# Keys and values of both attention branches as one 512-column product, and an indexer whose queries 1 to 3 are taken from rounded planes

## What is computed

```python
qa, ka, va, qb, kb, vb, iq, ik, iw, ga, gb = jnp.split(jnp.dot(h, w_in), IN_SPLITS, axis=-1)
dots = jnp.einsum('bqhd,bsd->bqhs', iq, ik) * IDX_SCALE
score = jnp.einsum('bqh,bqhs->bqs', iw * IDX_HEAD_SCALE, jax.nn.relu(dots))
_, sel = lax.top_k(score, topk)          # then attention b over the selected keys
```

## Time and profile before

| | us |
|---|---|
| median of three runs | 1031.42 |
| lowest and highest | 1030.24, 1037.22 |
| the profiled execution, its device time | 1036.8 |
| its span (first to last instruction) | 1035.0 |
| PE busy | 925.9 (89%) |
| DVE busy | 378.2 (37%) |
| ACT busy | 256.5 (25%) |
| mean granted clock of TensorE | 0.967 |

### The profile page before, as it was taken

The page is one execution under the profiler, slowest core; times in us unless marked ns, Lnnn a source line. Parts: engine busy times, 40 slices in busy tenths (PEclk is TensorE's granted clock), DMA queues, the critical chain, the costliest instruction groups (busy, mean ns, idle before and its releaser), DMA issues.

```text
span 1035.0 us, 14155 instructions
## 1 busy us (share of the span) xinstructions
PE 925.9 (89%) x5699; PEld 591.2 (57%) x5702; DVE 378.2 (37%) x974; ACT 256.5 (25%) x523; POOL 132.4 (13%) x136
## 2 busy tenths in 40 slices
PE   7989999999999999998999977877887888887996
PEld 7869995456999998994333322322322222234775
DVE  4179996764233436453111101101101011102796
ACT  6244326764323233221000000000000000001542
POOL 2403701113030000001111110011010110000000
PEclk9999998999999999997999999999999899999998
DMA  9850602002834316366999999999999999996601
GB/s 265 118 152 2 203 1 62 1 2 68 263 105 120 78 46 244 128 236 239 427 427 425 427 428 428 424 428 425 429 426 426 427 426 425 427 428 264 254 22 66
DMA packets 60132, 263.72 MB, mean 255 GB/s; under 512 B 11054, under 2 KB 36030, under 8 KB 46224
## 3 DMA queue, kind: packets, MB, share of 16 engines
q1 hardware_dynamic: 54160, 250.99, 63.0%
q0 software_dynamic: 5296, 9.79, 2.6%
q10 hardware_dynamic: 624, 2.23, 0.6%
HBM read 253.99 MB, written 16.85 MB: 262 GB/s over the span
## 4 chain that ended last, share of the span: by engine, by line
PE 63%; DMA 29%; DVE 4%; ACT 2%; issue 1%; SPq 1%; DVEq 0%; ACTq 0%
DMA arena<-in_w_up 25%; PE ps L1111 13%; PE ps L1278 12%; PE ps L980 5%; PE ps L1143 4%; PE ps L1426 4%; PE ps L1303 3%; PE ps L881 3%; PE ps L952 3%; DMA arena<-in_w_ple 2%; PE ps L1044 2%; PE ps L1014 2%; PE ps L1065 2%; PE ps L1399 1%; PE ps L1172 1%
## 5 line engine op out<-in xcount | busy, mean ns | idle before, releaser
L1278 PE MATMUL ps<-arena,hT 128*64 128x512 f32 x960 | 234.5, 641 | 39.4 <-DMA arena<-in_w_up 39.2
L1278 PEld LDWEIGHTS ps<-arena,hT 128*64 128x64 f32 x960 | 71.6, 141 | 199.3 <-issue 149.4
L2211 DVE TENSOR_TENSOR xf<-xf,ps 128x256 f32<-128x256 f32 x32 | 13.5, 421 | 401.6 <-ACT xf L1699 379.1
L1111 PE MATMUL ps<-arena_merge,arena_merge 128*128 128x256 f32 x624 | 99.7, 287 | 0.0
L1303 PE MATMUL ps<-arena,xf 128*64 128x512 f32 x336 | 76.7, 598 | 12.8 <-DVE xf L2214 12.8
L1111 PEld LDWEIGHTS ps<-arena_merge,arena_merge 128*128 128x128 f32 x624 | 87.4, 188 | 0.0
L836 POOL DMA_INDIRECT expert_rows<-xf,arena x32 | 32.2, 1007 | 425.6 <-ACT xf L1703 399.8
L1111 PE MATMUL ps<-xf_merge,arena_merge 128*128 128x256 f32 x480 | 82.0, 288 | 0.0
L1699 ACT ACTIVATE xf<-ps 128x256 f32<-128x256 f32 x30 | 11.6, 385 | 259.1 <-PE ps L1278 259.1
L1111 PEld LDWEIGHTS ps<-xf_merge,arena_merge 128*128 128x128 f32 x480 | 69.3, 188 | 0.0
L1703 ACT ACTIVATE xf<-ps 128x512 f32<-128x512 f32 x30 | 17.9, 598 | 159.8 <-PE ps L1303 159.8
(11 more groups left out here) (309 smaller groups left out, 1311.1 us busy)
## 6 DMA issues: line engine op xcount, KB each, us to landing
arena<-in_w_gate SPq DMA_DIRECT2D x30, 2048.0 KB, 29.4
arena<-in_w_up SPq DMA_DIRECT2D x30, 2048.0 KB, 37.0
arena<-in_w_down SPq DMA_DIRECT2D x11, 2048.0 KB, 36.4
hT<-in_w_down SPq DMA_DIRECT2D x11, 2048.0 KB, 36.5
arena<-in_w_down SPq DMA_DIRECT2D x20, 1024.0 KB, 32.2
arena<-in_w_in SPq DMA_DIRECT2D x10, 1024.0 KB, 6.2
arena<-in_w_in SPq DMA_DIRECT2D x3, 2048.0 KB, 10.5
arena<-in_w_gate SPq DMA_DIRECT2D x8, 512.0 KB, 9.0
```

Source lines behind the costliest of these rows:

```text
L1111: mm = pe.matmul(w[:, 2 * lo_t:lo_t + hi_t], rounded(st[:, c, cols]), rounded(mv[:, c, lo_t:hi_t]), start=c == 0 and k == 0, stop=c == pla ...
L1278: mm = pe.matmul(ps[g * BLK:(g + 1) * BLK, 2 + s, :], xsT[:, c, col:col + BLK], expert_columns(k, slice(0, 2), c, g), start=c == 0, stop=c ...
```

## The change

1. `iq` 1 to 3 are made in rounded planes (`index_queries` on PE) instead of float32. ACT makes their three high planes (`iq_hi`) ahead of that of `kvb`, and POOL their low planes. `iq` 0 stays a float32 product.
2. The order is now `iq` 0, `ikw`, `iq` 1, `ikT` p, `iq` 2, `ikT` s, `iq` 3, `dots`, on all engines. The first `dots` waits for `iq` 3 instead of `ikT` s.
3. ACT makes the high plane of `kva` between its readings of `ikT` s and of `iq` 3, instead of behind the dots. SP loads `kva` as soon as `ikw` is full, ahead of `qb`.
4. Keys and values of both branches are one product of 512 columns per tile, with one ring use (`('kv', t)`) instead of two. ACT reads a tile in two instructions. The sample's sums stand behind the second tile. PE waits for ACT's last tile once, and then makes all four groups of transposes.
5. ACT makes the high planes of `qb` ahead of its readings of the `kv` tiles, not behind the keys of branch b.

```diff
-    [(('xT', t), 'dve') for t in range(TILES)] + [(('iq', m), 'dve') for m in range(4)]
-    + [(('ikT', s), 'dve') for s in 'ps']
+    [(('xT', t), 'dve') for t in range(TILES)] + [(('iq', 0), 'dve'), (('iq', 1), 'dve'), (('ikT', 'p'), 'dve')]
+    + [(('iq', 2), 'dve'), (('ikT', 's'), 'dve'), (('iq', 3), 'dve')]
...
-    + [(('kvb', t), 'act') for t in range(TILES)] + [(('kva', t), 'act') for t in range(TILES)], 2)
+    + [(('kv', t), 'act') for t in range(TILES)], 2)
...
+    iq_hi = [None] + [at(kb, [KD, P]) for kb in (97.25, 101.25, 105.25)]
+    kv_lo2, kv_hi2 = at(16, [2, KD, 256]), at(32.5, [2, KD, 256])
...
+        sp.wait_ge(narrow_full, NARROW[('ikw', 4)].fill)
+        load(slab_kva, w_in[:, :, C_KVA:C_KVA + 256], slab_in['kva'])
         sp.wait_ge(wide_full, WIDE[('iq', 3)].fill)
         load(slab[0], w_in[:, :, C_QB:C_QB + 512], slab_in['qb'])
-        sp.wait_ge(wide_full, WIDE[('ikT', 'p')].fill)
-        load(slab_kva, w_in[:, :, C_KVA:C_KVA + 256], slab_in['kva'])
-        sp.wait_ge(narrow_full, NARROW[('kva', 4)].fill)
+        sp.wait_ge(narrow_full, NARROW[('kv', 4)].fill)
         load(slab[1], w_in[:, :, C_QA:C_QA + 512], slab_in['qa'])
...
-        pool.wait_ge(sw_high, 1)
+        for m in range(1, 4):
+            pool.wait_ge(sw_high, m)
+            low_of(slab[0][:, :, m * P:(m + 1) * P], slab[0][:, :, m * P:(m + 1) * P], iq_hi[m], "front").then_inc(sw_split, 1)
+        pool.wait_ge(sw_high, 4)
         low_of(slab_kvb, slab_kvb, kv_hi['b'], "front").then_inc(sw_split, 1)
+        pool.wait_ge(sw_high, 5)
+        low_of(slab_kva, slab_kva, kv_hi['a'], "front").then_inc(sw_split, 1)
...
+        def index_queries(m):
+            w = wide(open_slot(WIDE, ('iq', m), wide_out))
+            pe.wait_ge(f_split, KD)
+            for k in range(3):
+                if k == 2:
+                    pe.wait_ge(sw_split, m)
+                for c in range(KD):
+                    st = slab[0][:, c, m * P:(m + 1) * P] if k == 2 else iq_hi[m][:, c, :]
+                    mv = hT_lo if k == 1 else hT_f
+                    for a in range(2):
+                        mm = pe.matmul(w[:, a * 512:a * 512 + HALF], rounded(st, "front"),
+                                       rounded(mv[:, c, a * HALF:(a + 1) * HALF]),
+                                       start=c == 0 and k == 0, stop=c == KD - 1 and k == 2)
+            mm.then_inc(wide_full, 1)
+
+        pe.wait_ge(sw_high, 3)
+        index_queries(1)
...
-        pe.wait_ge(wide_out['dve'], WIDE[('ikT', 's')].out)
+        index_queries(3)
+        pe.wait_ge(wide_out['dve'], WIDE[('iq', 3)].out)
...
+        pe.wait_ge(sw_split, 5)
+        for t in range(TILES):
+            slot = open_slot(NARROW, ('kv', t), narrow_out)
+            for c in range(KD):
+                for k, (st, mv) in enumerate(((hT_f, kv_hi2), (hT_f, kv_lo2), (hT_lo, kv_hi2))):
+                    mm = pe.matmul(by_half(ps[0:ROWS[t], 6 + slot, :]), rounded(st[:, c, tok(t)]), rounded(mv[:, :, c, :], "front"),
+                                   start=c == 0 and k == 0, stop=c == KD - 1 and k == 2)
+            mm.then_inc(narrow_full, 1)
+            if t == 1:
+                sample_sums()
+        pe.wait_ge(narrow_out['act'], NARROW[('kv', 4)].out)
...
+        act.wait_ge(slab_in['iq'], 16)
+        for m in range(1, 4):
+            high(iq_hi[m], slab[0][:, :, m * P:(m + 1) * P], "front").then_inc(sw_high, 1)
         act.wait_ge(slab_in['kvb'], 16)
         high(kv_hi['b'], slab_kvb, "front").then_inc(sw_high, 1)
...
+        index_keys('s', NP, PAST + NS)
+        act.wait_ge(slab_in['kva'], 16)
+        high(kv_hi['a'], slab_kva, "front").then_inc(sw_high, 1)
+        index_queries(3)
...
-        act.wait_ge(slab_in['kva'], 16)
-        high(kv_hi['a'], slab_kva, "front").then_inc(sw_high, 1)
+        act.wait_ge(slab_in['qb'], 16)
+        query_weights_high(slab[0], qb)
+        for t in range(TILES):
+            slot, r = close(NARROW, ('kv', t), narrow_full), ROWS[t]
+            act.activation(kv_b[0:r, t, :], ps[0:r, 6 + slot, 256:512], ACT.Copy)
+            act.activation(kv_a[0:r, t, :], ps[0:r, 6 + slot, 0:256], ACT.Copy).then_inc(narrow_out['act'], 1)
```

More of the change, by code:

```diff
@@ L767, in query_weights_low @@
                 low(s[:, 4:8, m * P:(m + 1) * P], q_hi(dst, m, 1), "front").then_inc(sw_split, 1)
-        query_weights_low(3, slab[0], qb)
-        pool.wait_ge(narrow_out['act'], NARROW[('kvb', 4)].out)
+        query_weights_low(6, slab[0], qb)
+        pool.wait_ge(narrow_out['act'], NARROW[('kv', 4)].out)
         for nm, c in (('new_k', 0), ('new_v', P)):
@@ L909, in _ @@
         pe.wait_ge(wide_out['dve'], WIDE[('xT', 4)].out)
-        for m in range(4):
-            slot = open_slot(WIDE, ('iq', m), wide_out)
-            project(slot, lambda c: slab[0][:, c, m * P:(m + 1) * P], P, None, 0).then_inc(wide_full, 1)
+        slot = open_slot(WIDE, ('iq', 0), wide_out)
+        project(slot, lambda c: slab[0][:, c, 0:P], P, None, 0).then_inc(wide_full, 1)
         pe.wait_ge(slab_in['ikw'], 16)
@@ L945, in _, with sample_sums @@
         pe.wait_ge(f_split, KD)
[L946 to L960 removed]
+        def sample_sums():
+            w = wide(open_slot(WIDE, 'sums', wide_out))
+            pe.wait_ge(relu_used, 3 * HEADS + KV)
+            for lo, hi in ((0, PAST), (PAST, PAST + NS)):
+                mm = pe.matmul(w[0:NS, lo:hi], ident_s, score_s[:, lo:hi], start=True, stop=True)
+            mm.then_inc(wide_full, 1)
+        pe.wait_ge(sw_split, 5)
[9 more added lines that the diff above has]
+        pe.wait_ge(narrow_out['act'], NARROW[('kv', 4)].out)
+        for br, kv_n in (('b', kv_b), ('a', kv_a)):
             w = wide(open_slot(WIDE, ('k' + br + 'T', 'p'), wide_out))
[L962 removed]
             for t in range(4):
@@ L1888, in _, with index_keys @@
             ins.then_inc(wide_out['dve'], 1)
+        def index_keys(i, part, lo, cols):
+            w = wide(close(WIDE, ('ikT', part), wide_full))
+            dve.wait_ge(ik_high, i + 1)
+            dve.tensor_tensor(rounded(ikT[:, lo:lo + cols], "front"), w[:, 0:cols],
+                              rounded(ik_hi[:, lo:lo + cols], "front").bitcast(F32), ALU.subtract).then_inc(wide_out['dve'], 1)
+        index_queries(0)
         for t in range(TILES):
@@ L1896, in _ @@
             dve.tensor_scalar(iw_n[0:r, t, :], src[:, HD:IKW], IW_SCALE, None, ALU.mult).then_inc(narrow_out['dve'], 1)
-        for i, (part, lo, cols) in enumerate((('p', 0, NP), ('s', NP, PAST + NS))):
-            w = wide(close(WIDE, ('ikT', part), wide_full))
-            dve.wait_ge(ik_high, i + 1)
-            dve.tensor_tensor(rounded(ikT[:, lo:lo + cols], "front"), w[:, 0:cols],
-                              rounded(ik_hi[:, lo:lo + cols], "front").bitcast(F32), ALU.subtract).then_inc(wide_out['dve'], 1)
+        index_queries(1)
+        index_keys(0, 'p', 0, NP)
+        index_queries(2)
+        index_keys(1, 's', NP, PAST + NS)
+        index_queries(3)
         dve.wait_ge(narrow_out['dve'], NARROW_DONE['dve'])
```

45 lines of the change are left out of this document (11 added, 34 removed).

## The result

| | before | changed |
|---|---|---|
| median of 11 runs, us | 1035.39 | 1043.10 |
| lowest and highest, us | 1030.24, 1038.30 | 1039.38, 1046.89 |
| span of the profiled execution, us | 1035.0 | 1041.1 |
| mean granted clock of TensorE | 0.967 | 0.956 |

The changed kernel is slower: the ratio of its time to the time before is 1.0087, with a 95% interval of 1.0065 to 1.0109, so 9.0 us (6.7 to 11.3). The forecast was 1035.5 us, in a range of 1029.0 to 1040.5.

What follows compares the result with a forecast made beforehand. Up to attention, PE's and DVE's chains from the first dots were taken to bound it, 0.73 us apart. Dots 4.8 us later put attention +4.1 us: 1031.42 + 4.1 = 1035.5 us, range 1029.0 to 1040.5.

Steps and rivals of the forecast that it cites:

- The sum: DVE's chain at 165.9 us releases attention instead of at 161.84, +4.1 us, with nothing behind it changed.
- The wait for kva: ACT before reading iq 3: kva lands at 61.8 us behind the store, so dots start at 66.6, 4.8 us later.
- Rival A: SP's load of kva passes the store and lands before 55.4 us; attention 2.2 us early, 1029.2 us; chance 0.12.
- B: Rival: kva lands only at 66.8 us, dots 9.8 us late, attention 9.1, total 1040.5 us; chance 0.08.
- kva's low plane on POOL ends near 68.3, before kv at 84.: POOL's low plane around the start of dots, counted as free because keys and values need it only later.
- The small stall: PE inside ikw waits about 1.4 us for a narrow slot, vanishing in the wait for kva.
- The planes: Indexer queries iq 1 to 3 on PE: 6.06 us each instead of 7.38, saving 4.0 us, lost in PE's wait.
- The dots: Indexer dots stage: paced by DVE, low clock before too, length taken as unchanged.
- rival C: PE's wait costs TensorE's clock, sample's dots 4 us longer, 1039.5 us; slower by over 1% if longer; chance 0.05.
- Keys and values: PE's 512-column products behind the dots: 27.3 us instead of 28.66, gain 1.4 us, 1.1 after an added wait.
- D: Rival: the wide keys-and-values product gains nothing, attention +4.8 us, 1036.2 us; chance 0.75 together with the main forecast.
- The base: Whole kernel: the difference was put on the median 1031.42 us, the profiled execution being 0.5% above it.

Runs made afterwards that it cites:

- e6: Changed kernel, with the load of kva issued on ACT's queue at the same point, the store to toeplitz left on SP's queue; ratio to the kernel before 1.0087.
- e2: Changed kernel, with DVE's four small copies and the reduction moved ahead of its reading of iq 3; ratio to the kernel before 1.0046.
- e3: Changed kernel, with POOL's low plane of kva started only after DVE's first multiply-add on dots; ratio to the kernel before 1.0088.
- e4: e1 plus ACT reading iq 0 ahead of making the high plane of kvb; ratio to the kernel before 0.9978.
- e5: e4 plus DVE's copies moved behind its reading of ikT p, and dots started before iq 3 is read; 1031.20 us, ratio to the kernel before 0.9961.
- e8: Changed kernel, with only ACT's reading of iq 0 moved ahead of kvb's high plane, the store in its old place; one run, 1046.53 us.
- e1: Changed kernel, with SP issuing the store to toeplitz behind the loads of kva and qb; ratio to the kernel before 1.0024.
- e9: e5 with iq 1 to 3 as float32 products again, without their high and low planes; ratio to the kernel before 1.0008.
- e10: Kernel before the change, with DVE's four small copies and the reduction moved behind its last ikw tile; ratio to the unedited kernel 0.9999.
- a0: Changed kernel measured again without any edit, beside e1 to e3; 1044.09 us, ratio to the kernel before 1.0069.

## Why the prediction was off

**The effect, term by term.** The sum gave +4.1 us at attention, and +7.50 came. Of the 3.4 between them 0.9 are kva's later landing, 2.0 are DVE's copies, which had no term, and 0.5 are a gain behind the dots of which less came (0.3 us instead of 0.7). The range missed for one more reason, the base.

**The wait for kva: right, and 1.0 us short.** The prediction had kva land at 61.8 behind the store, ACT's high plane there, and dots at 66.6. They are 62.8 and 67.47, so +5.74 instead of +4.84. From kva's landing to the dots it gave 4.8 us and it took 4.66. The step that was short is the landing, worked out as 59.1 plus 2.7: the store landed at 59.3, and kva 3.4 us behind it, in other executions up to 4.4. Its reason, an order within the queue, is not needed, since another queue waits as long (e6); that the figure was near is in part luck. Rival A, that kva passes the store, is refuted; what it quotes is on the order of completion, not on a load that overtakes a store. B, a landing at 66.8, did not come.

**The failed step: "kva's low plane on POOL ends near 68.3, before kv at 84."** That asks only who needs the result, and costs the instruction at nothing. It ran from 64.80 to 69.31, and DVE had copies at 67.45. The trace before has them beside the first dots (61.59 and 61.73), so the prediction's own times, dots at 66.6 and POOL up to 68.3, laid one on the other. They took 2.73 us instead of 0.66, on DVE's chain and, through the dots, on PE's. The first multiply-add comes 3.13 us behind the first dots instead of 1.11: +2.02. With the 5.74 this is the whole +7.76. e2 and e3 show POOL as the cause; that 0.3 of it belong to POOL's issue of a store rather than to its low plane is read from the trace alone.

**The small stall: right in place, wrong in price, and hidden.** 1.4 us were forecast and 1.10 came. What it cost besides was a clock of 0.50 behind it: with the stall ikw takes 3.3 us longer than the 8.38 of e4, e5 and e8 (in e1 4.9), and the first instructions of iq 1 another 1.1. So PE was done with iq 3 at 59.88 and not at 57.3, and waited 7.59 us instead of 9. The prediction let it "vanish" in the wait for kva; in the changed kernel it does (e8), in a kernel where kva is in time it does not (e1 against e4).

**The planes: right.** 4.0 us forecast, 3.95 measured (e9 against e5), and in the changed kernel all of it lost in the wait.

**The dots, and rival C: right, refuted.** From first to last multiply-add it is 18.37 us before and after, although the granted clock was 0.50 up to about 75.8. The keys and values started at full rate. The measured time lies above C's 1039.5, but what C named did not bring it there.

**Keys and values: 1.4 us forecast, 0.45 came.** The 120 instructions of 512 columns take 11.33 + 16.88 = 28.21 us, 0.235 each, not the 0.227 of the earlier trace rows; before they took 28.66. From the first of them to the first of qb it is 32.09 us against 32.36, a gain of 0.27 instead of 1.1. The other traces agree: from the first multiply-add to attention it is 99.22 and 99.26 us with two products (before, e10) and 98.95 to 98.97 with one (the changed kernel, a0, e1, e4, e5, e6, e8, e9; in e2 and e3 POOL lies on multiply-adds of that stretch). D, put in the forecast's own range, was nearer. So PE's chain was again the longer one. DVE was done at 169.03 and ACT's last reading released the memset at 169.34, where the prediction had DVE release attention. That is why 7.76 at the scores became 7.50 at attention, and no less.

**The base.** The sum was put on a median of three runs, 1031.42. Eleven runs of the kernel before give 1035.39. Of the 7.6 us between forecast and result 4.0 are this, and 3.6 are the effect (7.7 by the medians instead of 4.1). The profiled execution, at 1036.8, had stood nearer to the later median than the one I scaled to. My range allowed for no error of the base: moved up by these 4.0 us it would have ended at 1044.5 and held the 1043.10, with the copies still at nothing. With the right base the number would have hidden the failed step. I had given only 0.05 to slower by more than 1%; the measured 0.87%, with its interval to 1.09%, lies at that bound. And that a measurement can't tell a difference under 1% from none was wrong: the interval is 0.2% to either side.

## What to carry to other kernels

When an operation of POOL moves, ask what DVE does in the same microseconds as well as who needs the result: here a small copy, and an operation with both operands in SBUF, lasted until POOL's end. Before a load is put ahead of work in an engine's order, look at what the DMA engines carry then. Here a store of small pieces held even the load on another queue, and moving that store was worth 4.7 us by the ratios of a0 and e1, more than the 4.0 of the planes or the 0.3 of the wide product. And a range needs the spread of the base in it, beside that of the effect.

## What the hardware showed that I had not expected

- Under a POOL instruction of 4.51 us one copy of 32x2 elements takes 1.88 us instead of 0.16, and under one of 4.75 us one multiply-add of 128x256 takes 4.62 instead of 0.48: each ends with POOL's instruction, to 0.3 us, and those beside it keep their time. A DVE subtraction that reads PSUM keeps its 0.73 us.
- A store in pieces of 1.5 KB at 102 GB/s, with a DMA share of 0.90, let no byte of another queue's load pass in the 13 us from 41 to 54. The load came through in the last five us of the store and the two behind them.
- A stall of TensorE of 1.10 us among instructions of 72 columns was followed by a granted clock of 0.50 over continuous work, for some 7 us in the changed kernel and some 10 in e1. In e4, e5 and e8, without that stall, the same 80 instructions took 8.38 us. With the clock's part of iq 1 the stall of 1.10 us cost 4.4 and 6.1 us.
- The fp32r product of 512 columns took 0.235 us each and that of 256 columns 0.119. A wide product saved 1.6% of its time.
